# Delta phase: the filling projections between level halves dealt out in six stretches of two instead of ten of one or two

## The chip, the cores and the metric

The kernel runs as one program on one core of a Trainium2 chip. The metric is the device time of one execution in microseconds (us); lower is better. Matrix products run on TensorE (PE in the profile; its weight loads are PEld), elementwise work on VectorE (DVE), ScalarE (ACT) and GpSimd (POOL), and the transfers are issued by SyncE (SP).

## The reference

The reference is a three-block sequence model over 512 tokens of width 1024. Its first block contains a mixer whose second half is a gated delta rule with four heads of 128 keys and 128 values. The sequence is cut in chunks, and inside a chunk a unit lower triangular system is solved:

```
a_mat = jnp.where(strict, bc[..., :, None] * kk * decay, 0.0) + jnp.eye(L)
rhs = jnp.concatenate([vc * bc[..., None], kc * (bc * jnp.exp(G))[..., None]], -1)
sol = lax.linalg.triangular_solve(a_mat, rhs, left_side=True, lower=True, unit_diagonal=True)
...
v_new = u_ - w_ @ state
o = qd_ @ state + attn_ @ v_new
state = gl_ * state + kd_.T @ v_new
```

Before it, the inputs q, k, v and a gate of each head come from a projection of the 512 tokens (1024 by 128 weights for each of the four), a short causal convolution and a silu. The rest of the model (another recurrent mixer, convolutional feed-forward blocks, attention) is not touched here.

## The kernel before

Everything is kept transposed, features on the 128 partitions and the 512 tokens along the free side, in eight tiles. The phases of the model are functions that run one after the other; the change lies in `delta`, which takes from about 140 to 290 us of the trace. A head's 512 tokens are four chunks of 128.

One projection (a head's q, k, v or gate; s = 0, 1, 2, 3 in the code) is eight **units**, one for each tile of input features. A unit is three products of 128 by 128 weights with 128 by 512 activations, since weight and activation are each split in a high and a low part (lines L190 to L192). Head h is worked on in `body(h)` while the gate and v of head h+1 (list `units`) and, later, q and k of head h+2 (`chunk_units`) are projected, unit by unit, between its steps.

The triangular matrix is inverted by doubling: six levels after the first. A level has two halves, each a block of small matmuls on TensorE. The first half, called **Y** below, multiplies the present inverse (`g_T`) with a band of the matrix (`g_BT`) into bank 4; ScalarE copies the result to `g_Y` (L2494; L2497 and L2499 for the last two levels). The second half, **Z**, multiplies `g_U` with that copy into bank 6; VectorE subtracts it from `g_T` (L2743) and transposes the new `g_T` into `g_U` (L2745). Then the next level's Y can go. Levels 1 to 4 have 32 by 32 tiles (L2227, sixteen of them and their weight loads in each half), level 5 is L2248 and L2257/L2258, level 6 is L2265 (Y) and L2272 (Z). After level 6 the recurrence over the four chunks begins with L2280.

TensorE executes strictly in the order in which the code issues. Between the halves the code calls `fill(l, i)`: `fill(l, 0)` stands between Y and Z of level l, that is while ScalarE copies; `fill(l, 1)` stands between Z of level l and Y of level l+1, that is while VectorE subtracts and transposes. The table `slots` says how many units each call issues; `give` takes them from the front of `units`. The gate's eight units come first, then v's. What is left of the sixteen after level 6 is issued in the recurrence, by `fill_chunk(0)` (all of the rest in heads 0 and 1) or one for each chunk (head 2). At level 4 the transposes of v (`turn_v`, L2185) also stand between Z and the next Y, at level 5 the two norm products (L2196, L2197) between Y and Z. Head 0 has projected four gate units already before its body, so its list holds twelve, and its entry (2, 0) is one. The last head has no units; it gets pieces of the output projection from `mix`, which does not use the table.

Of the kernel before, what the change touches and what calls it, by code (L numbers as in the profile page):

```python
# [2056 lines left out]
def delta(k, weights, out_tiles):  # L2057
# [80 lines left out]
    with nc.Block() as block:  # L2138
# [19 lines left out]
        def _(pe):  # L2158
            def project(s, h, lo, hi):

                for m in range(lo, hi):
                    if m == 0:
                        k.wait_split(pe, seq[s, h])
                        if s == 3:
                            pe.wait_ge(gate_taken, h)
                            if h >= 2:
                                pe.wait_ge(kdb_ready, h)
                            if h >= 3:
                                pe.wait_ge(y_ready, h - 2)
                        elif s == 2:  # L2170
                            pe.wait_ge(v_conv, h)
                        elif h == 1:
                            if s:
                                pe.wait_ge(qk_conv, 1)
                        else:
                            pe.wait_ge(at_ready if s else masked, h)
                    bank = qk1[s][0] if s < 2 and h == 1 else k.ps[s]
                    ins = k.product(bank[:, :], [x[:, m * P:(m + 1) * P] for x in k.ws[s]], [x[:, m, :] for x in (k.uh, k.ul)],
                                    m == 0, m == KD - 1)
                    if m == KD - 1:  # L2180
                        ins.then_inc(k.proj_done, 1)
# [11 lines left out]
            def norms(h):  # L2193
                bk, bq, _ = banks(h)
                pe.wait_ge(sq_ready, h + 1)
                nc.tensor.matmul(bq[:, :], k.c("ones"), k.sq[:, 0, :], start=True, stop=True)  # L2196
                nc.tensor.matmul(bk[:, :], k.c("ones"), k.sq[:, 1, :], start=True, stop=True).then_inc(nrm_qk, 1)  # L2197

            def keys(h):
                bk, bq, bt_ = banks(h)  # L2200
                pe.wait_ge(qk_ready, h + 1)
                four(bk, kk, kk)
                four(bq, kk, q).then_inc(kk_done, 1)
                if h:
                    pe.wait_ge(gate_taken, h + 1)
                turn(bt_, kk).then_inc(k_turned, 1)

            def turn_o(h):
                pe.wait_ge(on_scaled, h + 1)
                if h == H - 1:  # L2210
                    pe.wait_ge(s_ready, 3 * H)
                elif h == H - 2:
                    pe.wait_ge(masked, H)
                else:
                    pe.wait_ge(kdb_ready, h + 3)
                turn(b_out(h), on).then_inc(o_turned, 1)

            def turn_v(h):
                pe.wait_ge(v_silu, h + 1)
                pe.wait_ge(at_ready, h + 1)  # L2220
                turn(b5, v).then_inc(v_turned, 1)
# [9 lines left out]
            def level(h, l, fill):  # L2231
                pe.wait_ge(bt_ready, 4 * h + l)
                pe.wait_ge(t_ready, t_at(h, l - 1))
                blockwise(b4, BT[:, l - 1, :], Tc).then_inc(y_done, 1)
                fill(l, 0)
                pe.wait_ge(y_copied, y_at(h, l))
                if l > 1:
                    pe.wait_ge(u_ready, u_at(h, l - 1))
                else:
                    pe.wait_ge(*((s_ready, 3 * h) if h else (kdb_ready, 1)))  # L2240
                blockwise(b6, Uc, Yc).then_inc(z_done, 1)

            def level_32(h, fill):
                A = Ats[h % 2]
                pe.wait_ge(t_ready, t_at(h, 4))
                for c in range(NT):
                    for e, o in pairs:
                        ins = nc.tensor.matmul(b4[o, c32(c)], A[e, c * P + o.start:c * P + o.stop], Tc[e, c32(c)],  # L2248
                                               start=True, stop=True, tile_position=(e.start, o.start))
                ins.then_inc(y_done, 1)  # L2250
                fill(5, 0)
                pe.wait_ge(y_copied, y_at(h, 5))
                pe.wait_ge(u_ready, u_at(h, 4))
                for c in range(NT):
                    for e, o in pairs:
                        if e.start == 0:
                            nc.tensor.matmul(b6[o, c32(c)], Uc[o, c32(c)], Yc[o, c32(c)], start=True, stop=True, tile_position=(o.start, o.start))  # L2257
                        ins = nc.tensor.matmul(b6[e, c32(c)], Yc[o, c32(c)], Uc[o, c32(c)], start=True, stop=True, tile_position=(o.start, e.start))  # L2258
                ins.then_inc(z_done, 1)
# [48 lines left out]
            def mix(lo, hi):  # L2308

                for j, m in early_products[lo:hi]:  # L2310
                    if j == 0:
                        pe.wait_ge(*((y_ready, H - 1), (at_ready, H), (v_conv, H), (kdb_ready, H))[m])
                        if m == 3:
                            pe.wait_ge(y_ready, H - 2)
                    ins = out_tiles.product(pe, j, m)
                    if (j, m) in closing:
                        ins.then_inc(k.proj_done, 1)

            def body(h):
                n, f = h + 1, h + 2  # L2320
                units = [(s, n, m) for s in (3, 2) for m in range(KD)]
                slots = {(1, 0): 1, (1, 1): 1, (2, 0): 2, (2, 1): 1, (3, 0): 1, (3, 1): 1, (4, 0): 1, (5, 1): 2, (6, 0): 1, (6, 1): 1}
                if h == 0:
                    units, slots[2, 0] = units[4:], 1
                chunk_units = [(s, f, m) for s in (0, 1) for m in range(KD)]

                def give(n):
                    for s, g, m in units[:n]:
                        project(s, g, m, m + 1)
                    del units[:n]  # L2330

                def fill(l, i):
                    if n == H and (l, i) > (1, 0):
                        lo = 2 * l + i - 3
                        mix(lo, lo + 1)
                    if n < H:
                        give(slots.get((l, i), 0))
                    if n < H and (l, i) == (5, 0):
                        norms(n)

                def fill_chunk(c):
                    if n == H:
                        mix(11 + 2 * c, 13 + 2 * c)
                    elif f == H:
                        give(1)
                    elif c == 0:
                        give(len(units))
                    else:
                        for s, g, m in chunk_units[5 * c - 5:5 * c if c < 3 else None]:
                            project(s, g, m, m + 1)  # L2350
                    if n < H and c == 0:
                        keys(n)
                    if c == 2 and 0 < h < H - 1:
                        turn_o(h - 1)

                level(h, 1, fill)
                fill(1, 1)
                level(h, 2, fill)
                if n == H:
                    turn_o(h - 1)  # L2360
                fill(2, 1)
                level(h, 3, fill)
                fill(3, 1)
                if n == H:
                    turn_v(h)
                level(h, 4, fill)
                fill(4, 1)
                if n < H:
                    turn_v(h)
                level_32(h, fill)  # L2370
                fill(5, 1)
                level_64(h, fill)
                fill(6, 1)
                recur(h, fill_chunk)
# [7 lines left out]
            for h in range(H):  # L2382
                body(h)
# [1160 lines left out]
```

## Time and profile before

| | us |
|---|---|
| median of 3 runs | 1698.5 (1695.92 to 1699.22) |
| the profiled execution's own time | 1695.94 |
| its span | 1694.0 |
| TensorE busy in the span | 1648.5 |
| mean granted clock of TensorE, share of full speed | 0.996 |

The span is from the first to the last instruction; some 2 us of the time lie outside of it. A matmul's busy time in the trace is longer than its distance to the next one, because matmuls overlap: products in a row of 128 by 512 show 0.39 us each but start every 0.23 us. The distance from start to start is therefore what is read below. In the rows a bracket such as [0.41 <-ACT g_Y L2494] is the idle time of the engine just before the instruction and what ended it; no bracket means no idle time.

### The profile page before, as it was taken

What the parts mean: (1) busy time and instruction counts of PE and PEld (TensorE: products, weight loads), DVE (VectorE), ACT (ScalarE), POOL (GpSimd) and SP (SyncE); (2) the same over time, 40 slices, a digit from 0 to 9 for tenths busy, and PEclk for the clock granted to TensorE, in tenths of its full rate; (3) what the DMA queues carried; (4) which work ended last, traced back from release to release, by engine and by line L of the source; (5) the groups of instructions that cost most, each with busy time, mean ns of one, the idle gap of its engine ahead of it and who ended that gap; (6) DMA issues with size and microseconds to landing.
All of it is one profiled execution on the core that took longest, in us unless ns stands there. A gap on an engine that the chain in (4) does not pass through costs nothing. (4 is left out here: it accounts for less than half of the span.)

```text
span 1694.0 us, 25191 instructions
## 1 busy us (share of the span) xinstructions
PE 1648.5 (97%) x9050; PEld 1317.2 (78%) x9050; DVE 1050.1 (62%) x1704; ACT 838.7 (50%) x1427; POOL 417.3 (25%) x305
## 2 busy tenths in 40 slices
PE   9998998999999999999999999999999999999997
PEld 6786776788888788778888887888888876766775
DVE  6637555676666633787776848766663367888343
ACT  6756556444333422565565645433342245456663
POOL 1444531101011200055555510101120003232331
PEclk9999999999999999999999999999999999999999
DMA  5312212323332333222212122333323332321221
GB/s 221 119 71 76 63 39 89 112 75 99 90 96 87 102 97 99 75 69 70 75 50 75 56 88 69 99 90 96 99 90 97 99 99 66 112 72 55 62 63 50
DMA packets 40377, 144.50 MB, mean 85 GB/s; under 512 B 4562, under 2 KB 4818, under 8 KB 39780
## 3 DMA queue, kind: packets, MB, share of 16 engines
q1 hardware_dynamic: 40292, 143.36, 26.7%
q8 instruction: 54, 0.88, 0.2%
q14 instruction: 31, 0.25, 0.1%
HBM read 141.21 MB, written 2.13 MB: 85 GB/s over the span
## 5 line engine op out<-in xcount | busy, mean ns | idle before, releaser
L190 PE MATMUL bank<-u_high,w_high 128*128 128x512 f32 x1556 | 636.1, 409 | 7.9 <-DVE y_mix L2770 1.8
L192 PE MATMUL bank<-u_high,w_low 128*128 128x512 f32 x1556 | 608.8, 391 | 0.0
L191 PE MATMUL bank<-u_low,w_high 128*128 128x512 f32 x1556 | 607.7, 391 | 0.0
L190 PEld LDWEIGHTS bank<-u_high,w_high 128*128 128x128 f32 x1556 | 292.8, 188 | 85.0 <-issue 22.1
L192 PEld LDWEIGHTS bank<-u_high,w_low 128*128 128x128 f32 x1556 | 292.6, 188 | 63.5
L191 PEld LDWEIGHTS bank<-u_low,w_high 128*128 128x128 f32 x1556 | 293.4, 189 | 56.7 <-issue 3.1
L154 ACT ACTIVATE w_high<-w_ring 128x1024 fp32r<-128x1024 f32 x228 | 239.0, 1053 | 185.9 <-PE bank L192 160.8
L163 DVE TENSOR_TENSOR w_low<-w_ring,w_high 128x1024 fp32r<-128x1024 f32 x175 | 221.3, 1269 | 159.8 <-ACT w_high L154 159.3
L163 POOL TENSOR_TENSOR w_low<-w_ring,w_high 128x1024 fp32r<-128x1024 f32 x53 | 130.0, 2460 | 351.8 <-ACT w_high L154 351.8
L928 ACT ACTIVATE conv_up<-bank,col_sb 128x512 f32<-128x512 f32 x88 | 68.6, 780 | 263.4 <-DVE bank L988 263.4
L1057 POOL TENSOR_TENSOR hidden<-conv_up 128x512 f32 x44 | 58.3, 1326 | 488.1 <-DVE conv_up L999 364.0
L988 DVE TENSOR_TENSOR bank<-bank,root_in 128x512 f32<-128x512 f32 x88 | 61.4, 698 | 128.4 <-PE bank L192 126.0
L190 PE MATMUL bank<-src_high_down,w_high 128*128 128x512 f32 x352 | 137.5, 391 | 3.3 <-DVE src_low_down L516 3.3
L191 PE MATMUL bank<-src_low_down,w_high 128*128 128x512 f32 x352 | 137.0, 389 | 0.0
L192 PE MATMUL bank<-src_high_down,w_low 128*128 128x512 f32 x352 | 137.0, 389 | 0.0
L1396 POOL TENSOR_TENSOR c_X<-c_k,c_dif 128x256 f32<-128x256 f32 x56 | 62.2, 1112 | 244.3 <-ACT c_dif L1287 244.3
L190 PEld LDWEIGHTS bank<-src_high_down,w_high 128*128 128x128 f32 x352 | 66.1, 188 | 19.4 <-issue 2.2
L998 DVE SCALAR_TENSOR_TENSOR conv_up<-bank,col_sb,conv_up 128x511 f32<-128x511 f32 x88 | 65.9, 749 | 17.7 <-ACT conv_up L928 13.5
L192 PEld LDWEIGHTS bank<-src_high_down,w_low 128*128 128x128 f32 x352 | 66.1, 188 | 13.7
L191 PEld LDWEIGHTS bank<-src_low_down,w_high 128*128 128x128 f32 x352 | 66.1, 188 | 13.5
L999 DVE SCALAR_TENSOR_TENSOR conv_up<-bank,col_sb,conv_up 128x510 f32<-128x510 f32 x88 | 65.9, 749 | 10.1 <-DVE conv_up L998 0.3
L1397 POOL TENSOR_TENSOR c_X<-c_q,c_dif 128x256 f32<-128x256 f32 x56 | 63.1, 1127 | 0.0
(442 smaller groups left out, 2095.8 us busy)
## 6 DMA issues: line engine op xcount, KB each, us to landing
w_ring<-ffn_up SPq DMA_DIRECT2D x88, 512.0 KB, 3.5
w_ring<-ffn_down SPq DMA_DIRECT2D x44, 512.0 KB, 3.5
w_ring<-c_in SPq DMA_DIRECT2D x32, 512.0 KB, 3.6
w_ring<-g_in SPq DMA_DIRECT2D x16, 512.0 KB, 3.8
w_ring<-m_in SPq DMA_DIRECT2D x12, 512.0 KB, 7.8
w_ring<-fox_in SPq DMA_DIRECT2D x12, 512.0 KB, 4.3
w_ring<-dsa_in SPq DMA_DIRECT2D x12, 512.0 KB, 3.5
w_ring<-ab_out SPq DMA_DIRECT2D x8, 512.0 KB, 3.6
```

What stands on the lines that cost most here:

```text
L154: self.nc.scalar.activation(self.ws[s][0][:, :], self.w[:, s, :], ACT.Copy).then_inc(self.w_high, 1)
L163: eng.tensor_tensor(low[:, :], self.w[:, s, :], high[:, :].bitcast(F32), ALU.subtract).then_inc(self.w_split, 1)
L190: nc.tensor.matmul(out, a[0], b[0], start=start, stop=False)
L191: nc.tensor.matmul(out, a[0], b[1], start=False, stop=False)
L192: return nc.tensor.matmul(out, a[1], b[0], start=False, stop=stop)
L928: nc.scalar.activation(cg[:, s, :], bank(i, s)[:, :], ACT.Identity, bias=coef(4 * i + s, 3), scale=coef(4 * i + s, 2)).then_inc(tap_done, 1)
L988: nc.vector.tensor_tensor(bank(i, s)[:, :], bank(i, s)[:, :], k.rn[:, :], ALU.mult).then_inc(taken, 1)
L998: ch.link(nc.vector.scalar_tensor_tensor(cg[:, s, 1:T], bank(i, s)[:, 0:T - 1], coef(4 * i + s, 1), cg[:, s, 1:T], ALU.mult, ALU.add))
L999: nc.vector.scalar_tensor_tensor(cg[:, s, 2:T], bank(i, s)[:, 0:T - 2], coef(4 * i + s, 0), cg[:, s, 2:T], ALU.mult, ALU.add).then_inc(con ...
L1057: nc.gpsimd.tensor_tensor(h[:, bass.ds(2 * i + s // 2, 1), :], cg[:, s - 1:s, :], cg[:, s:s + 1, :], ALU.mult).then_inc(mul_done, 1)
L1396: nc.gpsimd.tensor_tensor(x[:, :, 0, :], blocks(kk[:, :], b)[:, :, 0, :], d[:, :, 0, :], ALU.mult)
L1397: nc.gpsimd.tensor_tensor(x[:, :, 1, :], blocks(q[:, :], b)[:, :, 1, :], d[:, :, 1, :], ALU.mult).then_inc(x_ready, 1)
```

## The change

Only the table is changed. A head still issues the same units in the same order; twelve of them between the halves (eleven in head 0) before and after.

```
-                slots = {(1, 0): 1, (1, 1): 1, (2, 0): 2, (2, 1): 1, (3, 0): 1, (3, 1): 1, (4, 0): 1, (5, 1): 2, (6, 0): 1, (6, 1): 1}
+                slots = {(1, 1): 2, (2, 0): 2, (2, 1): 2, (3, 1): 2, (5, 1): 2, (6, 1): 2}
                 if h == 0:
                     units, slots[2, 0] = units[4:], 1
```

The order of TensorE's instructions in level 1 of head 1 (`bank3` is the gate's bank, `bank4` takes Y, `bank6` takes Z; lines with - are before, with + after):

```order
 L2301 MATMUL bank7<-g_vn,g_attn0 128x128
 L2227 MATMUL bank4<-g_T,g_BT 32x32 x16
-L190 MATMUL bank3<-u_high,w3_high 128x512
-L191 MATMUL bank3<-u_low,w3_high 128x512
-L192 MATMUL bank3<-u_high,w3_low 128x512
 L2227 MATMUL bank6<-g_Y,g_U 32x32 x16
 L190 MATMUL bank3<-u_high,w3_high 128x512
 L191 MATMUL bank3<-u_low,w3_high 128x512
```

The unit between Y and Z is gone from there; Z now follows Y directly, and the unit stands behind Z with the one that was there already.

Level 6 of head 0, still TensorE (`bank2` is v's bank, L2265 is Y and L2272 is Z):

```order
 L192 MATMUL bank2<-u_high,w2_low 128x512
 L2265 MATMUL bank4<-g_T_wide,x_res 64x64 x4
-L190 MATMUL bank2<-u_high,w2_high 128x512
-L191 MATMUL bank2<-u_low,w2_high 128x512
-L192 MATMUL bank2<-u_high,w2_low 128x512
 L2272 MATMUL bank6<-g_U_wide,g_Y_wide 64x64 x4
+L190 MATMUL bank2<-u_high,w2_high 128x512
+L191 MATMUL bank2<-u_low,w2_high 128x512
+L192 MATMUL bank2<-u_high,w2_low 128x512
```

Here too the unit moves from before Z to behind it. Heads 1 and 2 have the same at level 6. At level 3 and, from level 4 to level 2's end, the other two units move in the same manner. The instructions of the other engines and their order are the same.

## Rows read from the trace of the kernel before

**Rows 1.** The page: busy time of TensorE and its weight loads, share, instructions.
```profile
PE 1648.5 (97%) x9050; PEld 1317.2 (78%) x9050; DVE 1050.1 (62%) x1704; ACT 838.7 (50%) x1427; POOL 417.3 (25%) x305
```

**Rows 2.** Busy time (count) in stretches: length, PE, PEld, DVE, ACT, POOL; clock, DMA share, GB/s.
```profile
152.43:171.40 18.97, 17.27 (x354) 11.20 (x355) 11.87 (x27) 14.68 (x28) 12.18 (x10) 1.00 0.15 36
190.76:208.51 17.75, 17.75 (x358) 11.73 (x357) 10.52 (x25) 13.23 (x28) 6.17 (x6) 1.00 0.14 48
230.37:248.11 17.74, 17.74 (x357) 11.73 (x357) 10.57 (x25) 13.22 (x32) 5.29 (x4) 1.00 0.10 39
...
208.51:230.37 21.86, 21.86 (x125) 18.62 (x123) 11.49 (x23) 9.46 (x30) 11.09 (x8) 1.00 0.16 44
248.11:259.53 11.42, 11.00 (x77) 9.45 (x75) 5.60 (x15) 6.19 (x22) 4.50 (x6) 1.00 0.01 1
```

**Rows 3.** Timeline of TensorE, head 1, levels 1 and 2: start, duration, what.
```profile
190.76 0.45 PE L2227 MATMUL bank<-g_T,g_BT 32*32 32x32 f32 x32
191.14 0.50 PE L190 MATMUL bank<-u_high,w_high 128*128 128x512 f32 x1
...
192.05 0.45 PE L2227 MATMUL bank<-g_Y,g_U 32*32 32x32 f32 x32
...
193.32 0.45 PE L2227 MATMUL bank<-g_T,g_BT 32*32 32x32 f32 x32
...
195.29 0.45 PE L2227 MATMUL bank<-g_Y,g_U 32*32 32x32 f32 x32
```

**Rows 4.** Timeline, last head, level 1: Y, the copy and Z with no unit between.
```profile
259.53 0.45 PE L2227 MATMUL bank<-g_T,g_BT 32*32 32x32 f32 x32
...
260.06 0.28 ACT L2494 ACTIVATE g_Y<-bank 128x128 f32<-128x128 f32 x1
...
260.39 0.45 PE L2227 MATMUL bank<-g_Y,g_U 32*32 32x32 f32 x32 [0.41 <-ACT g_Y L2494]
```

**Rows 5.** Timeline of ScalarE in head 1: copies 1, 2 and 4.
```profile
191.29 0.28 ACT L2494 ACTIVATE g_Y<-bank 128x128 f32<-128x128 f32 x1 [3.74 <-PE bank L2227]
...
194.74 0.26 ACT L2494 ACTIVATE g_Y<-bank 128x128 f32<-128x128 f32 x1
...
199.64 0.28 ACT L2494 ACTIVATE g_Y<-bank 128x128 f32<-128x128 f32 x1 [0.45 <-PE bank L2227]
```

**Rows 6.** Timeline, head 1, level 6: Y, copy, Z, subtraction, recurrence.
```profile
205.60 0.68 PE L2265 MATMUL bank<-g_T_wide,x_res 64*64 64x64 f32 x8
...
206.32 0.38 ACT L2499 ACTIVATE g_Y_wide<-bank 64x256 f32<-64x256 f32 x1
...
207.10 0.68 PE L2272 MATMUL bank<-g_U_wide,g_Y_wide 64*64 64x64 f32 x8
...
208.51 0.83 PE L2280 MATMUL bank<-g_U_wide,x_res 128*128 128x128 f32 x6
```

**Rows 7.** Timeline, head 0: level 2's halves, level 6's copy and Z.
```profile
155.42 0.45 PE L2227 MATMUL bank<-g_T,g_BT 32*32 32x32 f32 x32 [0.37 <-DVE g_T L2743]
...
157.97 0.45 PE L2227 MATMUL bank<-g_Y,g_U 32*32 32x32 f32 x32 [1.20 <-ACT g_Y L2494]
...
169.56 0.38 ACT L2499 ACTIVATE g_Y_wide<-bank 64x256 f32<-64x256 f32 x1
...
169.99 0.68 PE L2272 MATMUL bank<-g_U_wide,g_Y_wide 64*64 64x64 f32 x8
```

**Rows 8.** TensorE's waits over 1 us in the last head's levels.
```profile
264.38 0.45 PE L2227 MATMUL bank<-g_Y,g_U 32*32 32x32 f32 x32 [1.02 <-ACT g_Y L2494]
...
267.23 0.50 PE L190 MATMUL bank<-u_high,w_high 128*128 128x512 f32 x1 [1.81 <-DVE y_mix L2770]
```

**Rows 9.** Busy time and granted clock, late in the last head's levels.
```profile
266.00:268.00 2.00, 0.77 (x3) 0.48 (x3) 1.97 (x5) 1.30 (x3) 0.00 (x0) 1.00 0.07 27
268.00:270.00 2.00, 2.00 (x36) 1.15 (x35) 0.29 (x1) 1.33 (x2) 0.00 (x0) 0.64 0.03 8
270.00:272.00 2.00, 2.00 (x36) 1.57 (x36) 1.18 (x3) 1.81 (x3) 0.00 (x0) 0.50 0.00 0
```

## The prediction

> **What bounds the kernel now.** I read the page first: TensorE is busy 97% of the span [rows 1], so whatever makes TensorE stand still or spend longer on the same work should show in the time, unless it stands still already at that place. Next I read the busy time by stretch, with the cuts laid at each head's first level and at the start of its recurrence [rows 2]. In heads 1 and 2 the levels take 17.75 and 17.74 us and TensorE has no idle time in them at all; the recurrence of head 1 (208.51 to 230.37) has none either. Head 0's levels, the first row, have 1.70 us of it (18.97 less 17.27), the recurrence of head 2, the last row, has 0.42 us. The level stages are therefore a chain on TensorE itself, and the units between the halves hide ScalarE's copies and VectorE's subtractions fully. Last I read the timelines for single distances from start to start, which the busy times don't give.
>
> **What the pieces cost.** In head 1 [rows 3], Y to Z with one unit between is 192.05 - 190.76 = 1.29 us, Z to Y with one unit 193.32 - 192.05 = 1.27 us; I take 1.28. Y to Z with two units is 195.29 - 193.32 = 1.97 us. A second unit in a stretch thus costs 1.97 - 1.28 = 0.69 us, which is three products at 0.23. A first unit costs more: the small block itself takes 0.38 us until the first product starts (190.76 to 191.14), and 1.28 - 0.38 = 0.90 us remain for the unit. The excess, 0.90 - 0.69 = 0.21 us, is the price of entering and leaving a stretch. So each stretch that goes saves 0.21 us. That is the gain in the change.
>
> The price is the copy laid bare. Where no unit stands between, Z must wait for ScalarE. The last head does just this at level 1, where the table gives it nothing [rows 4]: Y starts at 259.53, the copy at 260.06 for 0.28 us, Z at 260.39, of which TensorE was idle 0.41 us. Y to Z bare is 0.86 us. Against 1.28 this saves 0.42 us in that gap, and the unit costs 0.69 us in its new one: +0.27 us for each such move. The break-even would be a bare distance of 1.28 - 0.69 = 0.59 us, and 0.86 is well above it.
>
> The 0.86 holds only while ScalarE is free when Y ends. The edit bares the copies 1, 3, 4 and 6. Copy 1 in head 1 came after 3.74 us of idling and copy 4 after 0.45 us [rows 5], each 0.53 us behind its Y, as in the last head. Copy 3 has less work ahead of it than copy 4, which has a silu and a table load; I take it as free too. Only copy 2 was bound by ScalarE's own work (it has no bracket), but there two units stay between the halves: copy 2 ends at 195.00, Z was at 195.29 [rows 3], and the edit moves TensorE 0.27 us later here while ScalarE's chain starts from work at the head's beginning, so it gets more room, not less. The table load in front of copy 4 follows copy 3 and so keeps its distance to Y. I cost ScalarE's lateness at nothing in heads 1 and 2.
>
> At level 6 [rows 6] Y to Z with a unit is 207.10 - 205.60 = 1.50 us. The copy starts 0.72 us behind Y, lasts 0.38, and in rows 4 Z followed 0.05 us behind the copy's end: bare 1.15 us. That saves 0.35 us, and the unit behind Z costs 0.69 us, since L2280 started when its one unit was over (1.41 us behind Z, with VectorE's result ready about 0.2 us before): +0.34 us.
>
> **The sum by head.** Heads 1 and 2: three moves by 0.27 (level 1; level 3; level 4's unit to level 2's end) and one by 0.34 make 0.81 + 0.34 = 1.15 us each. Head 0 is different [rows 7]. Its level 2 is pinned from outside: Y waits for VectorE (0.37 us), which still works on convolutions, and Z for ScalarE (1.20 us). The gap before level 2 has room: the levels start at 152.43 [rows 2], and 0.86 + 1.97 us later is 155.26; Y starts at 155.42 all the same. That move costs 0. The two moves at levels 2 to 4 cost 0.27 each as before. At level 6 the copy came late, at 169.56, behind ScalarE's own chain of roots, and Z at 169.99 did not start when the unit was over but when the copy was: taking the unit out saves nothing, and behind Z it costs the full 0.69. Head 0: 0 + 0.54 + 0.69 = 1.23 us. Sum: 1.23 + 2 x 1.15 = +3.5 us.
>
> The transfers, the splits of weights, the norms' squares on GpSimd and the decay work hang on ScalarE's and VectorE's place in the same chain and move with it; the gate's last unit comes no later than before (still ahead of level 4's Y). In the recurrences TensorE is the bound [rows 2], so they have nothing to give back (of head 0's I take it by head 1's). The last head waits for ScalarE and VectorE up to 1.81 us [rows 8], but those wait in turn for TensorE's last products of head 2, so it should be moved as a whole.
>
> Bounds of the one unmeasured quantity, the bare distance. From below: no wait beyond the block's 0.38 us would make each move in heads 1 and 2 a gain of 0.21 us, 8 x 0.21 = 1.7 us, while head 0 would come to 0 - 0.42 + 0.69 = +0.3: together -1.4 us. From above: TensorE waits for the copy as long as in the last head's level 2, 1.02 instead of 0.41 us [rows 8], at each of the ten bared gaps that are not pinned already; 10 x 0.61 = 6.1 us more, +9.6. I take 0.86, the nearest row: same instructions, same place in the level.
>
> The profiled execution took 1695.94 us, so the sum makes 1699.5 of it. That execution lay 2.6 us under the median of the runs; the same +3.5 on 1698.5 gives **1702.0 us**, +0.21%. About 0.2% (3.4 us) is what a measurement of this kernel can tell from no change.
>
> **Rivals.** A, the clock falls more often. The new stillness is some eleven idle pieces of some 0.5 us among small blocks. In the last head the granted clock went from 1.00 to 0.50, that is from 2.4 to 1.2 GHz, after a stretch in which TensorE was busy 0.77 of 2 us [rows 9]. There it lasted some 3.4 us (a mean of 0.64 over 2 us is 1.4 us at half speed, then 2 us at 0.50), which costs up to 1.7 us. Once in each of three heads that is +5.1 on top: 1707.1 us. Against it: head 0's levels hold 1.70 us of idle time, a single wait of 1.20 among it, at a clock of 1.00 all through [rows 2, 7]. The Trainium skill, "TensorE: Matmul & The Clock Gate", section "A second HAM failure mode: psum-queue depth-cycling", says that frequent short pauses between groups of matmuls can make the clock swing between its levels. By that rule this rival would come about; the trace so far disagrees, since head 0 has such pauses and shows no swing.
>
> B, not slower: the waits are covered after all and the saved entries remain. Its place is the ten gaps; its price is the lower bound, -1.4 us: 1697.1. It decides from a bare distance below 0.59 us. For it: TensorE's order gives no proof that what happens in the last head happens here. Against it: copy 1 started 0.53 us behind Y in head 1 as well [rows 5], and a copy lasts 0.28, so 0.81 is reached before any signal returns.
>
> C, the loss arises and is given back in the last head. Its waits of 1.02 and 1.81 us [rows 8] could swallow up to 2.8 of the 3.5 us if what TensorE waits for there were set by something that doesn't move: +0.7, 1699.2. For it: those are the largest waits of the phase. Against it: their causes, the copy behind the normalization of head 2 and the gated output of head 2, come after head 2's last chunk.
>
> **Chances.** Forecast (+2.3 to +4.7): 0.68. A: 0.10. B: 0.08. C: 0.14. Within the forecast a little over half lies above 3.4 us, 0.37, and 0.31 under it; A adds 0.10 and stray from B and C 0.03: slower 0.50. Faster takes part of B and stray, 0.06. Within 0.2%: 0.44. The range: the forecast's own is 1700.8 to 1703.2; with the runs' own spread (3.3 us over three) and reaching toward C and half of A it is 1697.5 to 1706.
>
> **What would show it.** In the timeline of the changed kernel, Y to Z bare at 0.86 us with a bracket of about 0.41 us that names the copy, at levels 1, 3 and 4 of heads 1 and 2; 1.15 us at level 6; Z to Y at 1.97 us; 18.9 us from level 1 to L2280 in heads 1 and 2 (17.75 before) and 20.2 in head 0 (18.97); the recurrences' lengths unchanged; the last head's as well. Wrong would be a bare distance under 0.6, a level stage of a head at or under its old length, a clock under 1.00 between 150 and 250 us, or waits in the last head that are shorter by as much as the heads before are longer.

## The result

Over 20 runs of each, the changed kernel takes 1700.62 us (median; 1698.92 to 1701.97) and the kernel before 1696.28 us (1695.73 to 1699.62). The ratio is 1.0021, with a 95% interval of 1.0015 to 1.0028: slower by about 3.6 us, 0.21%. The two means (1700.56 and 1696.91 us) are 3.65 us apart, the medians 4.34 us. The forecast was +3.5 us and 1702.0 us. The absolute number came out 1.4 us lower: the first three runs of the kernel before, on which it was built, had a median 2.2 us above that of the twenty, and the medians then moved by 0.8 us more than forecast, which took a part of that back. That the absolute number came so near is in part luck; the differences are what the forecast stands on.

The profiled execution of the changed kernel took 1700.42 us, 4.48 us more than that of before. The stretches between the same two instructions of each head (first level's Y to L2280), then the recurrences of heads 1 and 2, and last the last head's levels; the columns are those of [rows 2], and the granted clock is the third number from the end:

```profile
152.59:172.80 20.21, 16.66 (x353) 11.52 (x354) 12.96 (x28) 14.83 (x28) 12.87 (x10) 1.00 0.17 49
192.14:211.06 18.92, 17.23 (x357) 12.05 (x357) 11.43 (x26) 13.57 (x30) 6.52 (x6) 1.00 0.13 44
232.92:251.84 18.92, 17.23 (x357) 12.05 (x357) 11.44 (x26) 13.24 (x32) 5.29 (x4) 1.00 0.09 35
211.06:232.92 21.86, 21.86 (x125) 18.62 (x123) 10.79 (x22) 9.12 (x28) 10.40 (x8) 1.00 0.15 45
251.84:263.25 11.41, 10.99 (x77) 9.45 (x75) 4.89 (x14) 6.17 (x21) 4.50 (x6) 1.00 0.01 1
263.25:286.15 22.90, 18.71 (x354) 12.55 (x354) 13.72 (x27) 17.11 (x40) 0.96 (x1) 0.85 0.33 107
```

Against [rows 2], head 0's levels are 20.21 - 18.97 = 1.24 us longer, head 1's 18.92 - 17.75 = 1.17 and head 2's 18.92 - 17.74 = 1.18: together 3.59 us. The two recurrences have kept their lengths to 0.01 us. In heads 1 and 2 TensorE, which had no idle time, now has 18.92 - 17.23 = 1.69 us of it each.

TensorE in head 1, levels 1 to 4, in the changed kernel (start, duration, what; small blocks and the first of the copies only, the rows of the units are left out). These answer to [rows 3]:

```profile
192.14 0.45 PE L2227 MATMUL bank<-g_T,g_BT 32*32 32x32 f32 x32
192.67 0.28 ACT L2494 ACTIVATE g_Y<-bank 128x128 f32<-128x128 f32 x1 [3.75 <-PE bank L2227]
193.00 0.45 PE L2227 MATMUL bank<-g_Y,g_U 32*32 32x32 f32 x32 [0.41 <-ACT g_Y L2494]
...
194.99 0.45 PE L2227 MATMUL bank<-g_T,g_BT 32*32 32x32 f32 x32
...
196.96 0.45 PE L2227 MATMUL bank<-g_Y,g_U 32*32 32x32 f32 x32
...
198.92 0.45 PE L2227 MATMUL bank<-g_T,g_BT 32*32 32x32 f32 x32
199.78 0.45 PE L2227 MATMUL bank<-g_Y,g_U 32*32 32x32 f32 x32 [0.41 <-ACT g_Y L2494]
...
201.75 0.45 PE L2227 MATMUL bank<-g_T,g_BT 32*32 32x32 f32 x32
202.60 0.45 PE L2227 MATMUL bank<-g_Y,g_U 32*32 32x32 f32 x32 [0.41 <-ACT g_Y L2494]
```

Y to Z, bare, is 0.86, 0.86 and 0.85 us, each with 0.41 us of idle time ended by ScalarE's copy. At level 1 the copy ends at 192.67 + 0.28 = 192.95 and Z starts 0.05 us later. Z to Y with two units is 1.99, 1.96 and 1.97 us. Level 6 of the same head, with the copy, answers to [rows 6], and its Y to Z is 1.14 us:

```profile
207.82 0.67 PE L2265 MATMUL bank<-g_T_wide,x_res 64*64 64x64 f32 x8
...
208.53 0.38 ACT L2499 ACTIVATE g_Y_wide<-bank 64x256 f32<-64x256 f32 x1
...
208.96 0.68 PE L2272 MATMUL bank<-g_U_wide,g_Y_wide 64*64 64x64 f32 x8 [0.47 <-ACT g_Y_wide L2499]
...
211.06 0.83 PE L2280 MATMUL bank<-g_U_wide,x_res 128*128 128x128 f32 x6
```

### The profile page after: what moved, and what is told of

The parts are those of the page before. It is cut to its first block and busy times, and to the rows that moved or that the text cites. A ratio compares the mean times of both kernels' runs of the same rounds, so it can differ in the third digit from the quotient of the medians.

```text
span 1698.6 us, 25191 instructions
## 1 busy us (share of the span) xinstructions
PE 1648.5 (97%) x9050; PEld 1318.9 (78%) x9050; DVE 1051.0 (62%) x1704; ACT 838.8 (49%) x1427; POOL 416.9 (25%) x305
```

## The experiments

Each edit is shown against the kernel before; the slower copies, further down, are made in both kernels. The length of a stage is read from busy time by stretch, between the same instructions as above.

**Level 6 alone.**

```
-                slots = {... (5, 1): 2, (6, 0): 1, (6, 1): 1}
+                slots = {... (5, 1): 2, (6, 1): 2}
```

> Only the unit between Y and Z of level 6 is moved behind Z; the rest of the table is as before. Theory (the bared wait for the copy costs more than the saved entry into a stretch): heads 1 and 2 take 18.09 us from level 1 to L2280 (17.75 before), head 0 takes 19.66 (18.97), together +1.4 us, ratio to before 1.0008. Rival (fewer stretches pay, the wait is covered): heads 1 and 2 take 17.54 us each, together +0.3 us or less.

Ratio 1.0013 [1.0004, 1.0022] (11 runs of it). The stages of heads 0 and 1:

```profile
152.77:172.41 19.64, 17.06 (x353) 11.28 (x354) 12.54 (x28) 14.80 (x28) 12.84 (x10) 1.00 0.18 50
191.77:209.86 18.09, 17.62 (x357) 11.81 (x357) 11.21 (x26) 13.56 (x30) 6.51 (x6) 1.00 0.14 47
```

The forecast was 19.66 and 18.09 us; head 2 shows 18.09 too. The interval of the ratio is too wide to check 1.4 us by itself; the trace does it. Level 6 makes 0.67 + 0.34 + 0.35 = 1.36 of the 3.59 us; what the inner levels add is the rest, 2.2 us.

**Driven further: level 2 bare as well.**

```
-                slots = {(1, 0): 1, (1, 1): 1, (2, 0): 2, (2, 1): 1, (3, 0): 1, (3, 1): 1, (4, 0): 1, (5, 1): 2, (6, 0): 1, (6, 1): 1}
+                slots = {(1, 1): 3, (2, 1): 3, (3, 1): 2, (5, 1): 2, (6, 1): 2}
...
-                    units, slots[2, 0] = units[4:], 1
+                    units, slots[2, 1] = units[4:], 2
```

> The change driven further: no unit between Y and Z at levels 1 to 4 and 6 either, three units behind Z of levels 1 and 2 (two in head 0's level 2). Theory: level 2's gap goes from 1.97 to 0.86 us and two units cost 1.38 elsewhere, 0.27 us more per head than the change: 19.19 us for heads 1 and 2; head 0 stays at 20.2, since its level 2 is held by VectorE and ScalarE. Together +4.1 us against before, ratio 1.0024. Copy 2 is just free of ScalarE's own work by my count (0.07 us), so a wait of up to 0.3 us more could come here. Rival (fewer stretches pay): five stretches beat six, under the change by 0.2 us for each head.

Ratio 1.0029 [1.0017, 1.0040] (7 runs). Heads 0 and 1, then Y and Z of head 1's level 2:

```profile
152.79:173.00 20.21, 16.39 (x354) 11.56 (x355) 12.96 (x28) 14.80 (x28) 12.86 (x10) 1.00 0.17 50
192.34:211.55 19.21, 17.11 (x358) 12.12 (x358) 11.96 (x26) 13.66 (x30) 6.54 (x6) 1.00 0.13 45
```
```profile
195.88 0.45 PE L2227 MATMUL bank<-g_T,g_BT 32*32 32x32 f32 x32
196.74 0.45 PE L2227 MATMUL bank<-g_Y,g_U 32*32 32x32 f32 x32 [0.41 <-ACT g_Y L2494]
```

19.21 us where 19.19 was forecast, and head 0 as long as under the change. Fewer stretches go on being slower, by the trace: 19.21 us against 18.92 under the change (the interval of this ratio overlaps that of the change). Copy 2 found ScalarE free, so level 2 bare is 0.86 us like the others.

**One product of three left in the bared gap.** A unit is issued in single products; the table counts those.

```
+                units = [(s, n, m, i) for s in (3, 2) for m in range(KD) for i in range(3)]
+                slots = {(1, 0): 1, (1, 1): 5, (2, 0): 6, (2, 1): 5, (3, 0): 1, (3, 1): 5, (4, 0): 1, (5, 1): 6, (6, 0): 1, (6, 1): 5}
...
+                    for i in range(3) if part is None else (part,):
+                        ins = nc.tensor.matmul(bank[:, :], w[i // 2], u[i % 2], start=m == 0 and i == 0, stop=m == KD - 1 and i == 2)
```

> The change's table counted in single products, with one product of the moved unit (a third of it) left between Y and Z in each of the four bared gaps, so there are ten stretches again. Theory (the copy's end sets Z, not TensorE's work): one product is free there, Y to Z stays 0.86 us (1.14 at level 6), and the gaps behind Z shrink by 0.23 us each: 18.00 us in heads 1 and 2, 19.52 in head 0, together +1.0 us against before, ratio 1.0006. Rival (an entry into a stretch always costs its 0.21 us, wait or not): Y to Z grows to about 1.07 us and heads 1 and 2 stay at 18.8 us, +3.3 us in all.

Ratio 1.0005 [0.9996, 1.0014] (11 runs). Head 1's stage, and its level 1 (here L2228 is the small block, L2180 the product and L2495 the copy):

```profile
191.24:209.27 18.03, 18.00 (x357) 12.04 (x357) 11.43 (x26) 13.33 (x28) 6.29 (x6) 1.00 0.14 46
```
```profile
191.24 0.45 PE L2228 MATMUL bank<-g_T,g_BT 32*32 32x32 f32 x32
191.63 0.50 PE L2180 MATMUL bank<-u_high,w_high 128*128 128x512 f32 x1
191.77 0.28 ACT L2495 ACTIVATE g_Y<-bank 128x128 f32<-128x128 f32 x1 [3.75 <-PE bank L2228]
192.10 0.45 PE L2228 MATMUL bank<-g_Y,g_U 32*32 32x32 f32 x32
```

With a product in it the gap is 192.10 - 191.24 = 0.86 us, the same as without. The product cost nothing there, and each gap behind Z became 0.23 us shorter: 18.03 us instead of 18.92 (18.00 forecast), with ten stretches again; head 0 took 19.50 (19.52 forecast). The rival, that each entry costs its 0.21 us wait or not and the stage stays at 18.8 us, is ruled out.

Note the trap in these rows. TensorE's busy time is now 18.00 of 18.03 us and the bracket is gone, yet Z still starts 0.05 us behind the copy's end (191.77 + 0.28 = 192.05), as in the bare gap; the product's busy time of 0.50 us covers the wait. Only the distance shows it.

**Two products of three left.** The same code with (1, 0), (3, 0), (4, 0), (6, 0) at 2 and (1, 1), (2, 1), (3, 1), (6, 1) at 4.

> The change's table in single products with two products of the moved unit left between Y and Z. Theory: the second product outlasts the copy, so TensorE sets Z again: Y to Z is 1.05 us (0.38 + 0.34 + 0.33), Z to Y with four products 1.51, the sum 2.56 as with three and three; heads 1 and 2 take 17.8 us, head 0 19.0 to 19.3, all of the loss gone with a third of the moved work still moved: ratio 1.0001. Rival (the loss is in the uneven split itself, in proportion to what was moved): a third of the 1.17 us stays, 18.14 us.

Ratio 1.0000 [0.9990, 1.0009] (10 runs). Heads 0 and 1:

```profile
152.97:172.18 19.21, 17.29 (x354) 11.20 (x355) 12.32 (x27) 14.82 (x28) 12.41 (x10) 1.00 0.14 41
191.56:209.32 17.76, 17.76 (x357) 11.73 (x357) 11.02 (x25) 13.22 (x28) 6.16 (x6) 1.00 0.15 48
```

Head 1 is back at the 17.75 of before with a third of each unit still moved, not at 18.14; head 2 takes 17.75 us. The loss of these two heads is not in the uneven split but in the part of the copy that is left uncovered. Its Y to Z at level 1 is 1.05 us, as forecast. Head 0 keeps 19.21 - 18.97 = 0.24 us of its loss, inside the 19.0 to 19.3 that was forecast: at level 6 its late copy still sets Z (1.69 us behind Y), so the product that was moved behind Z costs its 0.23 us in full.

**The copy made slower, under both tables.** First in two halves of 64 columns, then in four of 32 (the edit shown is the one in four pieces; either edit adds a line, so the copy is L2495 there).

```
-                    ins = nc.scalar.activation(Yc[:, :], b4[:, 0:NT * B], ACT.Copy)
+                    for c in range(NT):
+                        ins = nc.scalar.activation(Yc[:, c32(c)], b4[:, c32(c)], ACT.Copy)
```

> The change, with ScalarE's copy of levels 1 to 4 made in two halves of 64 columns instead of one of 128, which makes it longer by some 0.2 us (I expect 0.15 to 0.27). Theory (the bared gaps are set by the copy): Y to Z at levels 1, 3 and 4 grows by just as much, from 0.86 to about 1.08 us; heads 1 and 2 take about 19.55 us instead of 18.92, and level 2's gap with its two units stays 1.97. Rival (the 0.86 us is a fixed turnaround of TensorE between two small blocks): it stays 0.86.

> The kernel before with the same slower copy. Theory (there the unit covers the copy): the copy ends about 1.05 us behind Y, within the 1.28 us that the unit takes, so heads 1 and 2 stay at 17.75 us; only head 0's level 2, where TensorE waits for the copy already, and the last head's level 1, grow by the 0.2 us each. Rival (the copy is on the path in both tables): Y to Z grows there too and the two kernels stay 1.17 us apart in each head.

The dose was smaller than I had planned: the two halves take 0.34 us together instead of 0.28. The answer was as small. Under the change's table Y to Z is 0.92 us (192.77 - 191.85 in head 1) and heads 1 and 2 take 19.13 and 19.12 us, three times 0.06 and a few hundredths more; under the table of before they take 17.74 and 17.75. The ratios are 1.0023 [1.0014, 1.0033] and 1.0000 [0.9991, 1.0010] (10 runs each). So I took a larger dose:

> The halved copy was only 0.06 us longer (0.34 against 0.28 for the pair), a small dose. Here the change has the copy of levels 1 to 4 in four pieces of 32 columns; by the pair's step of 0.12 us that makes about 0.22 + 3 x 0.12 = 0.58 us, 0.30 longer. Theory: Y to Z at levels 1, 3 and 4 is 1.16 us, heads 1 and 2 take 18.92 + 3 x 0.30 = 19.8 us. Rival (a fixed turnaround of TensorE): 0.86 to 0.92 and 18.9 to 19.1 us.

> The kernel before with the copy in four pieces. Theory: the copy now ends about 1.11 us behind Y, still inside the 1.28 us that the unit takes, so Y to Z stays 1.28 and heads 1 and 2 stay at 17.75 us; head 0 grows by 0.3 us at level 2, where TensorE waits for the copy. The distance to the change in heads 1 and 2 is then 2.07 us a head instead of 1.17. Rival (the copy is on the path in both tables): both grow alike and the distance stays 1.17.

The change with four pieces, head 1: stage, then the copy and Z of level 1, whose Y starts at 194.41:

```profile
194.41:213.91 19.50, 17.25 (x358) 12.05 (x358) 11.39 (x26) 14.31 (x42) 6.53 (x6) 1.00 0.14 45
```
```profile
194.94 0.47 ACT L2495 ACTIVATE g_Y<-bank 128x32 f32<-128x32 f32 x4 [3.75 <-PE bank L2227]
...
195.46 0.45 PE L2227 MATMUL bank<-g_Y,g_U 32*32 32x32 f32 x32 [0.59 <-ACT g_Y L2495]
```

The table of before with four pieces, head 1:

```profile
190.66:208.41 17.75, 17.75 (x358) 11.73 (x358) 10.86 (x25) 13.94 (x40) 6.15 (x6) 1.00 0.15 49
```

The four take 0.47 us (0.58 was expected), 0.19 more than one. With the change, Y to Z is 195.46 - 194.41 = 1.05 us, 0.19 more than 0.86, and the stage 19.50 us, 3 x 0.19 = 0.57 more than 18.92. With the table of before it stays 17.75. The distance between the tables went from 1.17 to 1.75 us a head by a change to ScalarE's copy alone (2.07 was forecast, for a copy 0.30 us longer instead of 0.19). So the copy is on the path where the gap is bare and is not where a unit covers it; a fixed turnaround of TensorE is ruled out. The ratios were 1.0029 [1.0019, 1.0040] and 1.0005 [0.9995, 1.0015] (8 and 10 runs).

**The mirror: bare behind Z instead of before it.**

```
+                slots = {(1, 0): 2, (2, 0): 3, (3, 0): 2, (4, 0): 1, (5, 1): 2, (6, 0): 1, (6, 1): 1}
...
+                    units, slots[2, 0] = units[4:], 2
```

> The mirror of the change: the units behind Z of levels 1 to 3 go to between Y and Z, so that the next Y stands bare behind Z and waits for VectorE's subtraction; (1,0) 2, (2,0) 3 (2 in head 0), (3,0) 2, the rest as before. Theory: that side has the same shape. Z to Y bare is 0.87 us (0.53 until VectorE starts, 0.29 for it, 0.05 back), against 1.28 with a unit, and each unit costs 0.69 in its new gap: 0.28 us for each of three moves, 18.6 us in heads 1 and 2. Head 0 wins 0.40 at level 2 (its second unit lies in the wait for the copy) and loses 0.28 at level 3: 18.85. Together +1.6 us, ratio 1.0009. Rival (only ScalarE's copy is dear, VectorE's side can be bared): heads 1 and 2 at 17.75 or less.

Ratio 1.0011 [1.0002, 1.0021] (10 runs). Head 1's stage, then its level 3's Z and level 4's Y:

```profile
190.96:209.87 18.91, 17.38 (x357) 12.06 (x357) 9.87 (x25) 13.22 (x28) 6.16 (x6) 1.00 0.13 44
```
```profile
199.50 0.45 PE L2227 MATMUL bank<-g_Y,g_U 32*32 32x32 f32 x32
...
200.03 0.29 DVE L2743 TENSOR_TENSOR g_T<-g_T,bank 128x128 f32<-128x128 f32 x1 [1.55 <-PE bank L2227]
...
200.47 0.45 PE L2227 MATMUL bank<-g_T,g_BT 32*32 32x32 f32 x32 [0.51 <-DVE g_T L2743]
```

The shape is as forecast, the size was not: 18.91 us where I had 18.6. Z to Y bare is 0.97 us, not 0.87. The subtraction starts 0.53 us behind Z and lasts 0.29, as assumed, but TensorE follows 0.15 us behind its end, where it follows 0.05 behind ScalarE's copy [rows 4]. Three gaps at 0.10 us make the missing 0.3. VectorE's side is dearer to bare than ScalarE's. Head 0 took 19.04 us, 0.19 over the forecast; its bare gaps behind levels 2 and 3 are the same 0.97 us.

**Room in head 0.** The table of before, but for head 0:

```
-                    units, slots[2, 0] = units[4:], 1
+                    units, slots[1, 0], slots[1, 1] = units[4:], 0, 2
```

> The table of before, but in head 0 alone level 1's unit goes behind Z and level 2 gets two units between Y and Z, where TensorE stood still for 1.20 us waiting for the copy; the recurrence's first chunk then has no unit left. Theory: both places are held from outside, so head 0's levels still take 18.97 us, and the distance from L2280 to the key products (L2190) falls from 1.59 to about 0.97 us, held then by VectorE's unit-length scaling: 0.6 us faster than before, ratio 0.9996, which only the trace can show. Rival (the idle time in head 0 is not free room): its levels grow by up to 0.69 us and nothing is won.

The median is 1695.07 us over 11 runs, the ratio 0.9991 [0.9982, 1.0000]. The stage of head 0, then TensorE at its level 2 and behind L2280:

```profile
152.44:171.41 18.97, 17.84 (x357) 11.85 (x358) 11.87 (x27) 14.68 (x28) 12.19 (x10) 1.00 0.15 39
```
```profile
157.98 0.45 PE L2227 MATMUL bank<-g_Y,g_U 32*32 32x32 f32 x32 [0.51 <-ACT g_Y L2494]
...
171.41 0.83 PE L2280 MATMUL bank<-g_U_wide,x_res 128*128 128x128 f32 x6
...
172.38 1.16 PE L2190 MATMUL bank<-g_k 128*128 128x128 f32 x8
```

The stage has kept its 18.97 us with a unit more in it: the wait for the copy fell from 1.20 [rows 7] to 0.51 us. L2280 to the keys is 0.97 us, as forecast. From head 0's level 1 to head 1's it is now 190.25 - 152.44 = 37.81 us, against 190.76 - 152.43 = 38.33: half a microsecond won. Of the timed kernels this is the fastest. That it beats the change is clear; that it beats the kernel before lies at the edge of the interval, and its median is 2.05 us lower, more than the 0.5 us that the new table explains. Part of the rest goes with the clock. In the profiles the last head's levels, which the table does not touch, took 20.81 us at a granted clock of 1.00 here and 21.78 us at 0.92 before. The 29 runs of the kernel before beside which this one was timed took 1695.25 us on average where their mean granted clock was 0.998 and 1698.59 where it was 0.994; head 0's table had a mean clock of 0.9967 over its runs, the kernel before 0.9956. Compared at equal clock the difference shrinks to some 1.0 us. Whether the table has a part in the better clock isn't shown.

## Why the prediction was right

**The bared gap.** Forecast 0.86 us with 0.41 us idle, measured 0.85 to 0.86 with 0.40 or 0.41 at every bared gap of levels 1, 3 and 4. The price of a second unit, 0.69 us, holds as well: the gaps with two units are 1.96 to 1.99 us. Only behind head 0's level 1 (2.14 us, held by VectorE) and behind level 6 (2.10 us, a longer block) are they longer, as was forecast. Together the two prices are the +0.27 us of a move.

**The sum by head.** 1.23 + 1.15 + 1.15 us forecast, 1.24 + 1.17 + 1.18 measured. Head 0's exceptions came as stated: level 2's Y stands 2.99 us behind level 1's in both kernels, its Z 2.55 us later in both, and level 6's Y to Z is 1.70 us with a unit in it and without. Level 6 of heads 1 and 2 gave 1.14 us for 1.15.

**The break-even.** It was put at a bare distance of 0.59 us. No kernel had so short a copy, so the point itself was not reached; from the other side, the slower copies moved the loss by just what they moved the distance.

**Rival A, the clock.** In heads 0 to 2 the granted clock stays at 1.00 in the changed kernel and in all ten experiments, with up to 2.1 us of pauses in the levels of heads 1 and 2 (19.21 - 17.11, level 2 bare as well) and up to 4.2 us in those of head 0 (20.79 - 16.61, the change with four pieces), single ones of 0.4 to 1.6 us. The Trainium skill, "TensorE: Matmul & The Clock Gate", section "A second HAM failure mode: psum-queue depth-cycling", tells of a kernel in which frequent short pauses between groups of matmuls made the clock swing. In these heads no trace here shows it. But the clock did move where I had no term for it, and one sign on record did not come: the last head's levels, whose instructions are unchanged, were to keep their length, and took 22.90 us instead of 21.78. The changed kernel there, columns as above:

```profile
268.00:270.00 2.00, 1.04 (x36) 0.76 (x36) 1.93 (x3) 1.97 (x4) 0.00 (x0) 1.00 0.86 326
270.00:272.00 2.00, 1.05 (x3) 0.83 (x3) 1.97 (x5) 1.03 (x2) 0.00 (x0) 0.56 0.06 25
272.00:274.00 2.00, 2.00 (x36) 1.31 (x35) 0.01 (x1) 0.74 (x2) 0.00 (x0) 0.50 0.03 8
274.00:276.00 2.00, 2.00 (x36) 1.19 (x36) 0.56 (x3) 1.99 (x3) 0.00 (x0) 0.50 0.00 0
276.00:278.00 2.00, 2.00 (x40) 1.49 (x39) 0.62 (x2) 0.89 (x3) 0.00 (x0) 0.74 0.00 0
```

Some 1.8 + 2 + 2 + 1.0 = 6.8 us pass at 1.2 GHz (a mean of 0.56 over 2 us is 1.8 us at half speed, 0.74 is 1.0), against some 3.4 before [rows 9]. With 22.90 - 21.78 = 1.12 us it is the only place besides the three heads where a microsecond went in the profiled executions, and it is why they differ by more (4.48 us) than the runs do (3.6). It doesn't follow the number of bared gaps: in the profiles with one product left, with two left and with head 0's table this stage took 20.8 us, at a clock of 1.00; with level 2 bare as well it took 21.74, with the mirror 22.69, and the table of before with the copy in four pieces took 23.18 (a few tenths of that are the slower copy itself). What decides it is left open. Each kernel has one profile, and the mean granted clock differs from run to run of the same kernel (0.994 to 0.998).

**Rival B, not slower.** It is ruled out by the gap (0.86 us, not under 0.59), and the kernel driven further shows once more that fewer stretches cost time.

**Rival C, given back in the last head.** Its waits are the same, 1.04 us for the copy and 1.80 for the gated output, against 1.02 and 1.81 [rows 8]. The last head starts 263.25 - 259.53 = 3.72 us later, so nothing had been given back by then, and it gave nothing back itself.

**What was loose.** The bounds, -1.4 and +9.6 us, were far wider than a distance with a row of its own deserved. And one row was read past: in head 0 TensorE's Y comes at 155.42 [rows 7], 0.14 us behind the end of VectorE's subtraction, which is this row of the kernel before:

```profile
155.00 0.28 DVE L2743 TENSOR_TENSOR g_T<-g_T,bank 128x128 f32<-128x128 f32 x1
```

It did not enter this sum, since every gap behind Z stays covered, but the mirror's forecast missed by it.

## What to carry to other kernels

When filler work is spread over the gaps of a dependent chain, price a gap from start to start in three forms: bare, with one piece, with two. A piece may leave a gap only if bare plus the marginal piece is less than the filled gap (here 0.86 + 0.69 against 1.28, so it may not); what a gap needs is filler that just outlasts what it hides, here two products of three. Look for gaps that are held by something else, as in head 0: there filler is free, and a table that is nearly the same for all heads misses them.

## What the runs showed of the hardware

Where TensorE waited for ScalarE's copy, it started 0.05 us behind the end that the profile shows for it; where it waited for VectorE's subtraction, 0.15 us behind (both 128x128 f32, with the same block of small matmuls after them). A copy on ScalarE cut into pieces costs little by itself: 128 columns in one take 0.28 us, in two 0.34, in four 0.47. And a busy time without a bracket does not prove that a matmul did not wait: in the kernel with one product left, 18.00 of 18.03 us count as busy while the copy still sets the start of Z.
